# Order of the vector engine's square sums and residual steps in a two-block transformer kernel

## The reference, cut to what matters

```python
x_lat = x_lat + m_lat[:, 2] * rms_norm(y_lat, norm_g[i, 1])
h = modulate(rms_norm(x_lat, norm_g[i, 2]), m_lat[:, 3], m_lat[:, 4])
x_lat = x_lat + m_lat[:, 5] * rms_norm(sqrelu_mlp(h, mlp_w1[i], mlp_w2[i]), norm_g[i, 3])
```

## Time and profile before

| what | value |
|---|---|
| median of 3 timed runs | 3879.44 us (3868.05 to 3882.18) |
| the profiled execution's own time | 3873.84 us |
| span of the profile | 3872.2 us |
| TensorE busy | 3604.2 us, 93% |
| VectorE busy | 1861.2 us, 48% |
| ScalarE busy | 1161.3 us, 30% |
| mean granted TensorE clock | 0.966 of full |

### The profile page before, as it was taken

How to read it: one execution, slowest core, us unless ns; L and a number is a source line. 1 busy time by engine, 2 the same in 40 slices (tenths; PEclk the granted TensorE clock), 3 DMA queues, 4 the chain that set the end, 5 groups by cost and what they waited for, 6 DMA issues and landing times.

```text
span 3872.2 us, 44636 instructions
## 1 busy us (share of the span) xinstructions
PE 3604.2 (93%) x16718; PEld 2810.3 (73%) x16718; DVE 1861.2 (48%) x2665; ACT 1161.3 (30%) x1500; POOL 202.3 (5%) x372
## 2 busy tenths in 40 slices
PE   7999889999979998799989999889999999899998
PEld 3566679999975665587855666668876777778876
DVE  4554555435443333554445555557754443445433
ACT  2133433312312122433323332333323222333332
POOL 1110001001000000011100000001100000000000
PEclk9999989999989999899999999889999999999999
DMA  6211113323310111244521111025543222223222
GB/s 210 75 60 60 44 48 125 100 93 123 107 50 28 38 33 38 85 155 157 165 98 44 44 43 32 12 98 178 183 133 98 66 76 65 65 76 98 97 82 81
DMA packets 294647, 335.13 MB, mean 87 GB/s; under 512 B 16401, under 2 KB 264081, under 8 KB 294417
## 3 DMA queue, kind: packets, MB, share of 16 engines
q1 hardware_dynamic: 263568, 233.06, 18.9%
q0 software_dynamic: 29440, 96.49, 7.8%
q10 hardware_dynamic: 1537, 4.13, 0.3%
HBM read 331.55 MB, written 2.10 MB: 86 GB/s over the span
## 4 chain that ended last, share of the span: by engine, by line
PE 86%; DVE 6%; ACT 3%; issue 2%; DMA 2%; ACTq 0%; DVEq 0%; SPq 0%; POOLq 0%; POOL 0%
PE acc L705 63%; PE sc L705 6%; PE sc L1219 2%; DMA wring<-in_mlp_w 1%; PE sc L739 1%; PE acc L916 1%; PE sc L832 1%; PE sc L896 1%; PE acc L1219 1%; PE acc L1397 1%; PE sc L898 1%; DVE w_lo L2164 1%; DVE arena L1921 1%; PE acc L1094 1%; PE sc L736 1%
## 5 line engine op out<-in xcount | busy, mean ns | idle before, releaser
L705 PE MATMUL acc<-x_lo,w_hi 128*128 128x512 f32 (+1 forms) x2048 | 772.5, 377 | 31.4 <-DVE d_out_lo L2141 9.2
L2164 DVE TENSOR_TENSOR w_lo<-wring,w_hi 128x1024 fp32r<-128x1024 f32 (+1 forms) x368 | 412.5, 1162 | 542.0 <-ACT w_hi L1577 541.6
L1577 ACT ACTIVATE w_hi<-wring 128x1024 fp32r<-128x1024 f32 (+1 forms) x368 | 352.3, 1005 | 989.5 <-DMA wring<-in_mlp_w 478.7
L705 PEld LDWEIGHTS acc<-x_lo,w_hi 128*128 128x128 f32 x2048 | 389.2, 190 | 94.7 <-DVE w_lo L2164 26.3
L705 PE MATMUL acc<-hid_hi,w_hi 128*128 128x512 f32 (+1 forms) x1120 | 413.7, 369 | 27.0 <-DVE arena L2199 12.0
L705 PE MATMUL acc<-hid_hi,w_lo 128*128 128x512 f32 (+1 forms) x1120 | 410.5, 366 | 0.0
L705 PE MATMUL acc<-x_hi_holes,w_hi 128*128 128x512 f32 x704 | 279.3, 397 | 10.8 <-DVE x_lo L2170 9.0
L705 PE MATMUL acc<-x_hi_holes,w_lo 128*128 128x512 f32 x704 | 278.9, 396 | 0.0
L705 PE MATMUL acc<-hid_lo,w_hi 128*128 128x384 f32 (+1 forms) x768 | 272.4, 355 | 0.0
L705 PEld LDWEIGHTS acc<-hid_hi,w_hi 128*128 128x128 f32 x1120 | 212.2, 189 | 55.6 <-DVE arena L2199 15.5
L705 PE MATMUL acc<-x_hi_seq,w_hi 128*128 128x512 f32 x576 | 227.9, 396 | 11.5 <-DVE x_lo L2173 9.0
(11 more groups left out here) (386 smaller groups left out, 5833.9 us busy)
## 6 DMA issues: line engine op xcount, KB each, us to landing
wring<-in_mlp_w SPq DMA_DIRECT2D x64, 1024.0 KB, 5.4
rows_or_mod<-in_ada_w POOLq DMA_DIRECT2D x208, 256.0 KB, 3.2
wring<-in_ffn_up SPq DMA_DIRECT2D x44, 1024.0 KB, 5.1
wring<-in_ret_w_in SPq DMA_DIRECT2D x24, 1024.0 KB, 5.2
rstd<-in_ada_w POOLq DMA_DIRECT2D x88, 256.0 KB, 3.5
wring<-in_ffn_down SPq DMA_DIRECT2D x32, 704.0 KB, 4.4
wring<-in_gdn_w_in SPq DMA_DIRECT2D x16, 1024.0 KB, 5.9
tab<-in_ada_w POOLq DMA_DIRECT2D x40, 256.0 KB, 3.5
```

The source lines that it names most:

```text
L705: ins = pe.matmul(o, lhsT, rhs, start=start, stop=stop)
L1577: f(w_hi[s][:, c], wring[s][:, c], ACT.Copy).then_inc(w_high, 1)
L2164: tt(w_lo[s][:, c], wring[s][:, c], w_hi[s][:, c].bitcast(F32), SUB).then_inc(w_split, 1)
```

## The change

`residual` issues its instructions block by block: the multiplication of block b+1 goes between the multiplication and the addition of block b, and each addition waits for its own block's multiplication alone (`settle(1)`: all marked steps but the latest). `out_y` adds the square of block j right behind the evacuation of block j, for j from 1 to 6, where it added that of block j-1. In the last quarter of an MLP the additions of squares 1 to 4 stand behind the evacuation of unit 13 and those of 5 and 6 behind unit 14, where one stood behind each of the units 10 to 15. No arithmetic instruction is added or removed; 7 waits are added in each of the four residuals.

```diff
-    def settle(self):
-
-        v = self.n if self.it is None else self.it * self.per + (self.n + self.local)
+    def settle(self, but=0):
+
+        v = self.n - but if self.it is None else self.it * self.per + (self.n + self.local - but)
         self.eng.wait_ge(self.sem, v)
...
                 deviation_of(name)
+                st.did(tt(y[:, 0], y[:, 0], rstd[:, 0:n], MUL))
                 for b in range(DB):
-                    st.did(tt(y[:, b], y[:, b], rstd[:, 0:n], MUL))
-                st.settle()
-                for b in range(DB):
+                    if b + 1 < DB:
+                        st.did(tt(y[:, b + 1], y[:, b + 1], rstd[:, 0:n], MUL))
+                    st.settle(int(b + 1 < DB))
                     if n == T:
                         stt(xT[:, b, 0:CTX], y[:, b, 0:CTX], dcol[:, l, q, b, 1:2], xT[:, b, 0:CTX], MUL, ADD)
...
                     if j in (2, 4):
                         split_weights(stage, 0, j // 2 + 1)
-                    if j >= 2:
-                        add_square(name, j - 1, n)
+                    if 1 <= j < 7:
+                        add_square(name, j, n)
...
                             free(ins, S, u)
-                            if last and u >= 10:
-                                add_square(f"y{i}m", u - 9, n)
+                            for b in {13: (1, 2, 3, 4), 14: (5, 6)}.get(u, ()) if last else ():
+                                add_square(f"y{i}m", b, n)
```

## The result

The changed kernel took 3841.52 us in the median of 5 runs (3839.12 to 3848.39), the kernel before 3875.02 in 5 (3868.05 to 3882.18). The ratio is 0.9918, 95% interval 0.9900 to 0.9937: 0.8% faster. Run again later beside other kernels it took 3845.58 against 3875.65, ratio 0.9932 (0.9918 to 0.9946). Forecast was 3845.6.

A forecast was written before the change was run, and what follows sets the result against it. TensorE bounds the kernel nearly everywhere, standing still for VectorE near the end of two MLPs. Gains 8.5 + 7.8 + 6.4 + 4.5 + 0 + 0 + 3.0 = 30.2 us give 3843.6, plus 2.0 is 3845.6; range 3834 to 3859.

The forecast's parts named there:

- The pause and its cause: Last MLP quarter: moving additions frees unit 11's evacuation; TensorE's idle 6.70 us in y0m and 5.9 in y1m go.
- the part that the lower clock costs: Units behind the pause in the last MLP quarter: slower clock there goes, 1.8 us in y0m and 1.9 in y1m.
- What is late next: Unit 14 needs the last weight group, there in time with 5.7 us to spare in y0m, 2 in y1m.
- The norm sums: End of the square sum, four times: first matmul step directly behind the product, together 6.4 us.
- The residual: x ready block by block: 4.5 us gained behind y0m, 3.0 behind y1m, 0 behind y0, about 0 behind y1.
- the sum in which TensorE catches up: Behind y1m: eighth `gdn_gate` matmul starts at 11.4 us, nine matmuls remain, ending at 19.2; gain 3.3 us.
- The forecast's other bound: Behind y1m: TensorE never catches up, 15.8 us from 3.0, 18.8 or somewhat later at lower clock; gain 2.3 us.
- the clock rival: TensorE's sums behind y0m: lower clock eats the residual's gain; whole kernel at 3859 us, chance 0.10.
- the forecast's rule: Start of y1's MLP: mean clock falling from 0.75 to 0.55 over 6.9 us loses 1.4 us; half, 0.7, taken.
- The waits: Seven added waits per residual find their multiplication finished and other work already running on VectorE; cost 0.
- the bound of 3 us: Residuals: at worst each of 28 added waits costs 0.11 us, by lost overlap and a gap.
- The base: Whole kernel: middle of the changed runs taken 2.0 us above the profiled execution's forecast, 3845.6 instead of 3843.6.

The follow-up runs named there:

- e4: Changed kernel with the addition of square 1 put back behind unit 10 in each MLP: 3861.66 us, 15.5 us slower than the changed kernel.
- e2: Kernel before with only the residual issued block by block: 3868.20 us against 3876.68, ratio 0.9972.
- e5: Changed kernel with all six additions of an MLP's squares behind unit 15: 3863.44 us, 19 us slower than the changed kernel.
- e1: Kernel before with only the additions in the last quarter of each MLP moved behind units 13 and 14: 3853.01 us against 3876.68, ratio 0.9938.
- e7: Changed kernel with each block's multiplication directly ahead of its own addition, a wait between them: 3844.68 us, ratio 0.9924 to the kernel before.
- e8: Changed kernel with VectorE's clearing of y_mlp issued ahead of the residual at y0 and y1: 3838.19 us, ratio 0.9904 to the kernel before.
- e9: Changed kernel with y_mlp cleared by GpSimd instead of VectorE: 3840.06 us against the changed kernel's 3845.58 beside it.

## Why the prediction was right

*The pause and its cause.* Right in cause and size. The step was to read that the evacuation of unit 11 stood behind the addition of square 1, and that neither transfer nor weights hold unit 13. e4 shows it with one addition. 8.8 and 8.2 us went where 8.5 and 7.8 were forecast; the part that the lower clock costs was about 0.3 us too small in both. I took it from the 8.48 us of unit 15, which count the whole of its last matmul (0.34 us, where one follows the other every 0.174); its granted clock was 1.00. Units 11 to 14 now take 8.36 each.

*What is late next.* Nothing was. The last group was split by 1100.8 (the row of L2165 above, 1098.44 and 2.36), some 8 us ahead of unit 14, which began at 1108.5; 5.7 were worked out. The split begins when half of the group is rounded and ends 1.44 us behind the rounding, where the sum took 2.3, and the transfer took 5.1 us from issue to landing instead of 6.44. The closest place, y1m, had 2 us left: its split ended at 1969.65, and unit 14 began at about 1971.6.

*The norm sums.* 1.3, 3.0, 0.8 and 0.8 us where 1.4, 3.1, 0.95 and 0.95 were forecast. The single step takes 1.57 us, not half of 2.86: two steps in a row took 0.28 us less than twice one alone, all at a granted clock of 1.00.

*The residual.* Behind y0m 4.1 instead of 4.5. The step that was a little wrong is the end: the last two blocks of x come 1.07 us apart and not 1.93, as no multiplication stands between them (block 6 is ready at 1146.93), and the last sum then waits for the one before it. TensorE's last piece was 2.86 us for two blocks and not 1.29 for one:

```profile
1145.86 0.40 DVE xT L1926
1146.26 0.67 DVE xT L1927
1146.93 0.02 issue
1146.95 0.85 ACT sq L1449
1147.81 0.04 issue
1147.85 2.86 PE sc L736 x8
```

Behind y1m 3.3, where 3.0 were taken: the sum in which TensorE catches up gave 19.2 us from the residual's start to the end of `gdn_gate`, and measured are 19.2 (1987.49 to 2006.69). The forecast's other bound doesn't follow from its own numbers: 18.8 from 22.5 is a gain of 3.7, and the 2.3 beside it stand on a lower clock whose cost isn't worked out. At y0 nothing, as forecast, and at y1 1.0 us ahead of the clock.

*The clock.* The rival that e2 names fell, and TensorE's timeline behind y0m in the changed kernel shows how:

```profile
1136.29 9.27 PE L736 MATMUL sc<-sq,base_tab 128*128 128x384 f32 x20 [5.79 <-ACT sq L1449]
1145.92 1.56 PE L736 MATMUL sc<-sq,base_tab 128*128 128x384 f32 x4 [0.37 <-ACT sq L1449]
1147.85 2.85 PE L736 MATMUL sc<-sq,base_tab 128*128 128x384 f32 x8 [0.37 <-ACT sq L1449]
```

And these are the stretches (length, busy PE, PEld, DVE, ACT, POOL, granted clock, DMA):

```profile
1134.20:1140.60 6.40, 4.31 (x7) 2.47 (x8) 6.40 (x12) 2.53 (x3) 0.00 (x0) 0.50 0.06 22
1140.60:1150.80 10.20, 9.23 (x26) 4.28 (x25) 7.38 (x12) 4.28 (x6) 0.00 (x0) 1.00 0.00 0
```

The first sums run at 0.50 of the clock behind the pause of 5.79 us, the later ones at 1.00. At the lower clock a sum takes longer (2.55 us in the earlier trace rows, at 0.50) than the 1.93 us between two blocks of x, so the first five sums (x20) follow each other without a gap, and the clock rose in them: the first ones were slower than the blocks of x, the later ones faster, as the forecast took them. Only the last three are handed over with gaps, two of 0.37 us, and the clock stayed at 1.00 to the end. That so short gaps would be harmless in a longer row isn't shown by this stage. No run shows the clock rival's time either, the 3859 us to which the forecast stretched its range: the granted clock over these sums was 0.85 in the mean (1136.29 to 1150.70), and the changed kernel took 3841.52 and 3845.58 us.

The start of y1's MLP ran at a mean of 0.55 instead of 0.75:

```profile
1605.50:1612.40 6.90, 6.83 (x18) 5.38 (x19) 6.39 (x10) 6.74 (x11) 0.11 (x1) 0.55 0.47 152
```

That is 1.4 us by the forecast's rule, twice what I took off. That the longer pause ahead of it (6.5 us instead of 4.5) is the cause is not shown. In the first 6.9 us of this MLP the clock was 0.55 in three traces with a pause of 6.5 us (the changed kernel's two and e5), but 0.72 in e4 with one of 7.4 and 0.66 in e1 with one of 4.5. It is better taken as a spread of 1.4 us than as a cost.

*The waits.* 0 taken, 0 measured; the bound of 3 us is about the 3.6 that e7 costs, where each wait does find VectorE without other work.

*The base.* Adding 2.0 us to the profiled execution for the middle of the runs was of little moment: the two medians of the changed kernel, 3841.5 and 3845.6, lie on both sides of it.

## What to carry to other kernels

In an engine's in-order stream, look at a short instruction that waits for another engine, and ask what that engine is waiting for at the time: here a 0.96 us addition inherited the wait for a 1 MB transfer (6.44 us from issue to landing, and 17.90 us of ScalarE's idle time) by way of ScalarE's stream, and passed it on to TensorE by way of an evacuation queued behind it. Put such a step behind the last thing that others need, but not so late that its own turns outlast the work beside it, as in e5. When a chain of multiply and add per block feeds a consumer, issue it block by block with one multiplication ahead; here it paid 4.1 and 3.3 us behind y0m and y1m, where the consumer was the end, and 0.1 us behind y0, where the producer's own next work was; the multiplication ahead saved 0.12 us a block of 768 tokens (e7).

## What the runs showed of the hardware

- The 128x6144 clearing on VectorE was 5.18 us long and came after 1.23 us in which VectorE did nothing and waited for nothing that the profile shows; the 128x4096 one was 3.47 us and came after 0.80. All twelve traces with these clearings have the same four numbers, also that of e8, where they stand ahead of the residual. The pause is 0.20 ns per element of a row in both, pause and length together are 6.41 and 4.27 us, 1.04 ns per element in both. What VectorE does in the pause is not shown.
- GpSimd cleared 128x6144 in 5.21 us, beginning 0.06 us behind the evacuation that it waited for (e9), and VectorE's multiplication beside its last 0.94 us took 0.96 us, as it did in the changed kernel without it.
- Two matmul steps in a row took 2.86 us and one alone 1.57 (the changed kernel), both at a granted clock of 1.00, and two after an 11.6 us pause, at a granted clock of 0.50, 5.50.
